# Reordering the norm steps around two MLPs and merging the attention score operations

## The reference, cut to what matters

```
x  = x + rwkv(...) @ wo                      # "wo"
x  = x + relu(rms(x) @ w1)**2 @ w2           # "mlp0": 1024 -> 4096 -> 1024
k, v = rms(x) @ w_kv ; k = rms(k)            # "kv"
q  = rms(rms(x) @ wq)                        # "q", 16 heads of 64, 2 key heads
s  = q k^T - slope_h * distance, window 128  # distance outside the window: -inf
m  = max(max(s), sink_h)
p  = exp(s - m) / (sum exp(s - m) + exp(sink_h - m))
x  = x + (p v) @ b_wo                        # "bo"
x  = x + relu(rms(x) @ w1')**2 @ w2'         # "mlp1"
ctx  = modulated(rms(context)) @ w_in[:, 512:1536]
lat  = modulated(rms(x)) @ w_in              # "qk", then v, gates, Fourier part
```

## Time and profile before

| what | us |
|---|---|
| median of 3 runs | 2321.64 (2315.77 to 2322.67) |
| the profiled execution's own time | 2319.46 |
| its span, first to last instruction | 2317.7 |
| TensorE busy | 2145.5 (93%) |
| VectorE busy | 1227.5 (53%) |
| ScalarE busy | 800.4 (35%) |
| GpSimd busy | 158.7 (7%) |

### The profile page before, as it was taken

How to read it: one execution, slowest core, us unless ns; L and a number is a source line. 1 busy time by engine, 2 the same in 40 slices (tenths; PEclk the granted TensorE clock), 3 DMA queues, 4 the chain that set the end, 5 groups by cost and what they waited for, 6 DMA issues and landing times. The chain is left out here.

```text
span 2317.7 us, 34614 instructions
## 1 busy us (share of the span) xinstructions
PE 2145.5 (93%) x14072; PEld 1639.1 (71%) x14072; DVE 1227.5 (53%) x1784; ACT 800.4 (35%) x1312; POOL 158.7 (7%) x128
## 2 busy tenths in 40 slices
PE   6999999989999999888899999998998787999997
PEld 1667899927787787556668888886874365888885
DVE  5578565563534434547637557456342645556423
ACT  5766333322312212425532122225222323444311
POOL 0000222220101101000001011010000000000000
PEclk9999999969999999999999999999999898999998
DMA  4320000032232232220035534534320012232320
GB/s 173 111 79 31 3 4 4 5 136 73 90 102 91 82 109 79 67 70 1 19 109 177 195 137 138 189 129 138 125 82 0 9 64 91 91 105 94 136 91 36
DMA packets 58499, 200.76 MB, mean 87 GB/s; under 512 B 7936, under 2 KB 10752, under 8 KB 57344
## 3 DMA queue, kind: packets, MB, share of 16 engines
q1 hardware_dynamic: 57760, 194.17, 24.5%
q10 hardware_dynamic: 608, 4.72, 0.6%
HBM read 191.92 MB, written 6.42 MB: 86 GB/s over the span
## 5 line engine op out<-in xcount | busy, mean ns | idle before, releaser
L1067 DVE TENSOR_TENSOR wlo<-raw,whi 128x1024 fp32r<-128x1024 f32 x282 | 342.2, 1223 | 705.1 <-ACT whi L622 703.7
L622 ACT ACTIVATE whi<-raw 128x1024 fp32r<-128x1024 f32 x282 | 295.3, 1057 | 852.7 <-PE bank L1684 828.3
L1682 PE MATMUL bank<-inh,whi 128*128 128x512 f32 x1200 | 473.9, 395 | 37.8 <-DVEq L1617 16.1
L1683 PE MATMUL bank<-inl,whi 128*128 128x512 f32 x1200 | 471.3, 393 | 0.0
L1684 PE MATMUL bank<-inh,wlo 128*128 128x512 f32 x1200 | 470.9, 392 | 0.0
L1682 PEld LDWEIGHTS bank<-inh,whi 128*128 128x128 f32 x1200 | 228.0, 190 | 93.7 <-DVEq L1617 16.9
L1683 PEld LDWEIGHTS bank<-inl,whi 128*128 128x128 f32 x1200 | 227.8, 190 | 48.1 <-issue 0.7
L1684 PEld LDWEIGHTS bank<-inh,wlo 128*128 128x128 f32 x1200 | 227.9, 190 | 48.0
L1682 PE MATMUL bank<-hidh,whi 128*128 128x512 f32 x576 | 231.0, 401 | 10.1 <-DVE wlo L1067 4.5
L1683 PE MATMUL bank<-hidl,whi 128*128 128x512 f32 x576 | 228.4, 397 | 0.0
L1684 PE MATMUL bank<-hidh,wlo 128*128 128x512 f32 x576 | 228.0, 396 | 0.0
(11 more groups left out here) (351 smaller groups left out, 3003.2 us busy)
## 6 DMA issues: line engine op xcount, KB each, us to landing
raw<-in_mlp_w SPq DMA_DIRECT2D x128, 512.0 KB, 3.6
ADW<-in_w_ada SPq DMA_DIRECT2D x32, 768.0 KB, 5.2
raw<-in_w_up SPq DMA_DIRECT2D x44, 512.0 KB, 3.5
raw<-in_w_in SPq DMA_DIRECT2D x28, 512.0 KB, 3.6
raw<-in_a_w_rkv SPq DMA_DIRECT2D x24, 512.0 KB, 3.3
raw<-in_w_down SPq DMA_DIRECT2D x22, 512.0 KB, 3.4
raw<-in_a_wo SPq DMA_DIRECT2D x8, 512.0 KB, 5.9
raw<-in_b_wq SPq DMA_DIRECT2D x8, 512.0 KB, 3.2
```

The lines of the kernel that those rows point to most:

```text
L622: act.activation(whi[u % SLOTS][:, :], raw[u % SLOTS][:, :], ACT.Copy).then_inc(w_hi, 1)
L1067: dve.tensor_tensor(wlo[u % SLOTS][:, :], raw[u % SLOTS][:, :], whi[u % SLOTS][:, :].bitcast(F32), ALU.subtract).then_inc(w_lo, 1)
L1682: pe.matmul(o, w[:, wc], xh, start=start, stop=False)
L1683: pe.matmul(o, w[:, wc], xl_, start=False, stop=False)
```

## The change

ScalarE makes the high part of a block before its square, and after the first four squares the high parts of the later blocks go ahead of their squares (kv: two of them). TensorE makes the sums in two groups of four, after different units. VectorE makes the low parts of blocks 0 and 1 between the additions of `add_x` (after blocks 2 and 5). mlp0 is built like mlp1 (loop of two passes, turn c written out) and the drain behind it is gone. In mlp1's turn c the modulations run after three of eight splits, and SyncE's loads of `RC` and `CX` come behind the third weight load of the down pass. The retention states come after k = 2 instead of k = 1, with banks 2 and 3 between them and the wait for their eviction. In attention the gain of q is multiplied by 1/slope, the distances are negated, and one `tensor_tensor_reduce` for each half replaces L1402, L1409 and L1412: it writes (scores + band) times -slope and the minimum of that and -sink.

```diff
-    band = np.stack([first, band, band], 1)
+    band = -np.stack([first, band, band], 1)
...
+                    if layer == 1 and tag == "c" and j == 2:
+                        sp.wait_ge(dmo.sem, dmo.at(("sum", "c", CB - 1)))
+                        sp.wait_ge(rc_out, 16)
+                        sp.dma_start(RC[:], rsp).then_inc(rc_in, 16)
+                        sp.dma_start(CX[:], t["ctx"]).then_inc(in_ctx, 16)
...
-            def x_stats(name, prev, dst, gain, last_unit, root=True):
-
-                for kb in range(CB):
+            def x_stats(name, prev, dst, gain, last_unit, order):
+
+                for what, kb in order:
                     act.wait_ge(x_sum.sem, x_done(prev, kb))
-                    square_of(name, kb, X[:, kb, :])
-                    if kb == CB - 1:
-                        act.wait_ge(lin.sem, used(last_unit, None))
-                    gained_hi(name, dst, gain, kb)
-                if root:
-                    root_of(name, PB[0])
+                    if what == "square":
+                        square_of(name, kb, X[:, kb, :])
+                    else:
+                        if kb == CB - 1:
+                            act.wait_ge(lin.sem, used(last_unit, None))
+                        gained_hi(name, dst, gain, kb)
+
+            first_half = [(what, kb) for kb in range(4) for what in ("hi", "square")]
+            inputs_first = first_half + [("hi", kb) for kb in range(4, CB)] + [("square", kb) for kb in range(4, CB)]
+            squares_first = first_half + [("hi", 4), ("hi", 5)] + [("square", kb) for kb in range(4, CB)] + [("hi", 6), ("hi", 7)]
...
+                split_run(u0, 1)
+                root_of(name, PB[0])
...
-                    split_run(u + 8, 8, lp)
+                    split_run(u + 8, 3, lp)
+                    if layer == 1 and tag == "c":
+                        modulated_hi("ctx", chh, CT, lambda kb: adac[:, kb, 1:2], CTX)
+                    split_run(u + 11, 5, lp)
...
-                        act.activation(pb, pb, ACT.Exp, bias=st[:, b:b + 1], accum_out=st[:, 2 + b:3 + b]).then_inc(aat.sem, aat.step())
+                        act.activation(pb, pb, ACT.Exp, scale=-1.0, bias=st[:, b:b + 1], accum_out=st[:, 2 + b:3 + b]).then_inc(aat.sem, aat.step())
...
+                    if follow is not None and m in (2, 5):
+                        name, dst_h, dst_l, gain = follow
+                        gained_lo(name, dst_h, dst_l, gain, (m // 3,))
...
-            def mlp(layer, u0, name, at_end=None):
-                gained_lo(name, inh, inl, f"ln_mlp{layer}")
+            def mlp(layer, u0, name, at_end=None, follow=None):
+                gained_lo(name, inh, inl, f"ln_mlp{layer}", range(2, CB))
+                split_run(u0, 1)
...
-                    split_run(u + 8, 8, lp)
-                    if tag == "c":
+                    split_run(u + 8, 3, lp)
+                    if tag == "c" and at_end is not None:
                         at_end()
-                    add_x(nm, lp)
+                    split_run(u + 11, 5, lp)
+                    add_x(nm, lp, follow if tag == "c" else None)
...
-                    dve.scalar_tensor_tensor(S1[i % 3][:].rearrange("p (a b) -> p a b", a=2), BAND[:, nn:nn + 2, :],
-                                                        -(2.0 ** (-8.0 * (h + 1) / HEADS)),
-                                                        PB[i % 4][:].rearrange("p (a b) -> p a b", a=2), ALU.mult, ALU.add).then_inc(da.sem, da.step(("taken", i)))
-                    k = da.n
-                    dve.wait_ge(da.sem, k)
                     if i >= 4:
                         dve.wait_ge(da.sem, da.at(("den", i - 4)))
-                    dve.tensor_reduce(st[:, 8:10], S1[i % 3][:].rearrange("p (a b) -> p a b", a=2), AX.X, ALU.max).then_inc(da.sem, da.step())
-                    k = da.n
-                    dve.wait_ge(da.sem, k)
-                    dve.tensor_scalar(st[:, 0:2], st[:, 8:10], col("sinks", h), -1.0, ALU.max, ALU.mult).then_inc(da.sem, da.step(("nm", i)))
+                    for b in range(2):
+                        half = slice(b * 256, (b + 1) * 256)
+                        dve.tensor_tensor_reduce(S1[i % 3][:, half], PB[i % 4][:, half], BAND[:, nn + b, :], -(2.0 ** (-8.0 * (h + 1) / HEADS)),
+                                                 SINKM[:, h:h + 1], ALU.add, ALU.min, st[:, b:b + 1]).then_inc(
+                            da.sem, da.step(*([("taken", i), ("nm", i)] if b else [])))
...
-                             late=(0,), after={0: lambda: sums4(name, PB[0]), 1: lambda: total(name, PB[0])}, late_after=rooted)
+                             late=(rooted, 0), after={(0, 7): lambda: sums4(name, PB[0], range(4)), (1, 7): lambda: sums4(name, PB[0], range(4, CB)),
+                                                      (2, 4): lambda: total(name, PB[0])})
...
-            pe.drain().then_inc(phase, 1)
-            pe.wait_ge(phase, phase_done("pe"))
...
+                    if kb == 7:
+                        total("kv", PB[0])
...
-                if j == 1:
-                    sums4("kv", PB[0])
-                if j == 2:
-                    total("kv", PB[0])
+                if j in (1, 2):
+                    sums4("kv", PB[0], range(4 * j - 4, 4 * j))
...
-                if k == 2:
+                if k == 1:
                     pe.wait_ge(x_sum.sem, x_done("mlp1c", 4))
-                    sums4("lat", PB[4])
+                if k in (1, 2):
+                    sums4("lat", PB[4], range(4 * k - 4, 4 * k))
...
-            wide(UIN, inh, inl, "qk", ready=(dad, ("lo", "lat")), free=(x_sum, lambda m: x_done("mlp1c", m)), late=(0, 1, 2, 3), after={1: states}, late_after=states_taken)
+            wide(UIN, inh, inl, "qk", ready=(dad, ("lo", "lat")), free=(x_sum, lambda m: x_done("mlp1c", m)), late=(states, 2, 3, states_taken, 0, 1))
```

More of the change, by code:

```diff
@@ L1289, in split_run, with add_x @@
                     split_lo(u + 3, loop)
-            def add_x(stage, loop=None):
+            def add_x(stage, loop=None, follow=None):
                 for m in range(CB):
@@ L1346, in work @@
                     hidden_lo(7)
-                    split_run(u + 8, 8, lp)
-                    if tag == "c":
+                    split_run(u + 8, 3, lp)
+                    if tag == "c" and at_end is not None:
                         at_end()
-                    add_x(nm, lp)
+                    split_run(u + 11, 5, lp)
+                    add_x(nm, lp, follow if tag == "c" else None)
                 work("a", u0, None)
-                with turns(dve, "dve", name, 3 - layer, 16) as lp:
+                with turns(dve, "dve", name, 2, 16) as lp:
                     lp.first = u0 + 16
                     work("b", u0 + 16, lp)
-                if layer == 1:
-                    work("c", u0 + 48, None)
+                work("c", u0 + 48, None)
             split_run(UWO, 8)
-            add_x("wo")
-            mlp(0, UM0, "mlp0")
-            dve.drain().then_inc(phase, 1)
-            dve.wait_ge(phase, phase_done("dve"))
+            add_x("wo", follow=("mlp0", inh, inl, "ln_mlp0"))
+            mlp(0, UM0, "mlp0", follow=("kv", inh, inl, "kv_norm"))
             dve.memset(QNI[:], 0.0).then_inc(dk.sem, dk.step("qnz"))
-            gained_lo("kv", inh, inl, "kv_norm")
+            gained_lo("kv", inh, inl, "kv_norm", range(2, CB))
             split_run(UKV, 1)
@@ L1476, in _ @@
             split_run(UBO, 8)
-            add_x("bo")
+            add_x("bo", follow=("mlp1", inh, inl, "ln_mlp1"))
             def modulations():
@@ L1661, in _, with sums4 @@
             pn, pl = STEP["pe_norm"], STEP["pe_lora"]
-            def sums4(name, bank):
-                for kb in range(CB):
+            def sums4(name, bank, kbs):
+                for kb in kbs:
                     g = kb % 4
@@ L1937, in _, with wide @@
             dmlp = STEP["dve_mlp"]
-            def wide(u0, mh, ml, stage, loop=None, ready=None, free=None, zero=None, late=(), after=None, late_after=None):
+            def wide(u0, mh, ml, stage, loop=None, ready=None, free=None, zero=None, late=(), after=None):
+                banks = [m for m in late if isinstance(m, int)]
                 def block_(k, m):
@@ L1955, in wide @@
                     for m in (*range(1, CB), 0) if k == 0 and zero is not None else range(CB):
-                        if not (k < 3 and m in late):
+                        if not (k < 3 and m in banks):
                             block_(k, m)
-                    if after is not None and k in after:
-                        after[k]()
-                    if k == 2 and late:
-                        late_after()
+                        if after is not None and (k, m) in after:
+                            after[k, m]()
+                    if k == 2:
                         for m in late:
-                            for k2 in range(3):
-                                block_(k2, m)
```

(24 more changed lines are left out.)

37 lines of the change are left out of this document (16 added, 21 removed).

## The result

The changed kernel takes 2267.78 us (median of 4 runs, 2265.27 to 2269.51) where the kernel before takes 2320.47 (4 runs, 2315.77 to 2322.67): a ratio of 0.9773, 95% interval 0.9761 to 0.9785. The forecast was 2267 with a range of 2259 to 2284. The profiled execution took 2269.51 us, 1.7 above the median.

A forecast was written before the change was run, and what follows sets the result against it. TensorE, busy 93% of the span, was taken as the bound, with time to be had only in its waits. Savings of 8.4 + 8.4 + 4.9 + 12.9 + 19.8 = 54.4 us take the median from 2321.64 to 2267 us, range 2259 to 2284.

The forecast's parts named there:

- A: End of wo and start of mlp0: TensorE goes straight on, sums run in two groups without waits; 8.4 us saved.
- C: End of bo and start of mlp1: same steps as at mlp0; 8.4 us saved.
- B: From mlp0 over kv to q: drain goes, new waits of 0.6, 1.0 and 1.6 us; 4.9 us saved.
- a chain that the change leaves as it is: From kv's total to q's start: root, reciprocal, three low parts, splits; 8.3 us, unchanged.
- D: mlp1 to context and states: additions start earlier, k = 2 fills the gap at the states; 12.9 us saved.
- E: Attention loop: merged operations take a pair of iterations from 6.59 to 5.35 us, 16 pairs; 19.8 us saved.
- n: Attention: time from the first merged operation to the exponentials, taken as 1.0 us with 0.43 an operation.
- free chain: Attention: VectorE and ScalarE in turn, 3.32 + n + (n - 0.1) a pair, 5.22 us.
- the forecast's bound: Attention: a bound of TensorE's own, two pairs take at least 2n + 8.7, so 5.35 us a pair.
- Half rate (1): Attention: merged operation runs at half rate, 0.70 us each, only 4.6 us saved there; 2282 us, chance 0.13.
- A boundary that gives back (2): One stage boundary loses its gain to a new wait, late weight or low clock, 5 to 9 us; 2274, chance 0.15.
- Rivals 3 and 4: Attention: merged operations at 0.78 us each gain nothing, 2287, chance 0.05; at 1.68 each they lose 58, 2345, chance 0.03.

The follow-up runs named there:

- e7: Changed kernel with all low parts of the norm inputs behind the eight additions again, at mlp0, kv and mlp1: 2277.67 us, ratio 0.9816.
- e8: Changed kernel with all eight sums behind k = 0 and squares ahead of high parts again, at mlp0 and mlp1 alone: 2272.64 us, ratio 0.9794.
- e6: Changed kernel with the context input and the loads of context and reciprocal back at the end of turn c: 2275.26 us, ratio 0.9805.
- e11: Changed kernel with kv's sums after blocks 1 and 3, total ahead of block 5, copy of sums ahead of the split: 2259.56 us, ratio 0.9733.
- e1: Changed kernel with attention's merged operations put back to the three operations of before: 2283.63 us, ratio 0.9842.
- e10: Kernel before with attention's merged operations and their constants alone: 2300.73 us, ratio 0.9912.
- e2: Changed kernel with one merged operation more in each attention iteration, its results unused: 2274.85 us, ratio 0.9798.
- e3: Changed kernel with attention's low part issued one iteration later, behind that iteration's merged operations: 2258.82 us, ratio 0.9735.
- e9: Kernel before with attention's low part issued an iteration later, the three operations kept: 2310.49 us, ratio 0.9951.
- e4: Changed kernel with 16 merged operations more behind attention's last low part, sources in PSUM or SBUF, 256 or 512 wide: 2280.88 us, one run.
- e5: Changed kernel with kv's total one block earlier, ahead of block 6 and not of block 7: 2263.49 us, ratio 0.9751.

## Why the prediction was right, and where it was not

**A and C** (8.4 each): 8.0 and 8.7. From mlp0's first product to the end of the second sums the forecast had 11.8 us; it starts at 570.93, and the sums' successor at 582.77: 11.8. e7 and e8 take the gain apart: about 4.3 us from the low parts (2.5 of it the wait, the rest the clock) and 3 to 4 from the sums.

**B** (4.9): 3.4. All three waits came, as forecast: 0.58, 0.71 and 1.81 for 0.6, 1.0 and 1.6. The step that failed is the time of "a chain that the change leaves as it is". It took 947.18 to 956.37, 9.2 us for 8.3, since its first member, the total, ran behind the wait of 1.81 at the lower clock: 1.91 us instead of 1.02, and the root began that much later. I had priced the wait and not the clock behind it. But the wait alone doesn't settle the clock: of the nine profiles with the same wait of 1.81, e6 and e8 have the total at 1.02, the chain at 8.31 and a gain of 4.5 in kv's column. So 0.9 of the missing 1.5 go with where a stretch at the lower clock fell, and what puts it there is open. The other 0.6 are in the sum up to the total: taken from mlp0's end as in the forecast it came after 15.7 us for 15.1, though the three waits together were no longer than forecast. Each delays the next start by 0.1 to 0.2 us more than the idle shown for it, since the idle counts from the end of a matmul of 0.39 us whose successor could start after 0.23. e11 shows the chain at 8.3 too. The idle ahead of q was 5.27 for "about 6.4", and 5.89 in e6 and e8, where block 7's product ran at the full clock.

**D** (12.9): 14.4. The context's total came 1551.32 - 1537.98 = 13.3 us behind mlp1 for 13.2. The gap at the states shrank by 2.76, 3.28 to 0.52, for 2.7. Not in the sum was that the states' own 32 matmuls then take 3.81 us and not 5.22: the granted clock was 0.72 there before and is 1.00 now. `RC` and `CX` on SyncE's queue cost nothing that TensorE shows, as taken: it waits for no weight there.

**E** (19.8): 19.5 in the column. The operation's price was 0.40 for my 0.43, n 0.92 for 1.0, the pair 5.385 for 5.35. e1 and e10 show the term from both sides (18.0 and 20.5), and at equal clock it is 18.0, 1.8 under the forecast: all 16 pairs were priced like the steady ones, and the first three save less. That the column still shows 19.5 is luck, 1.5 us of it with the clock.

The mechanism was right: two chains, the later counts. The free chain of 5.06 over VectorE, ScalarE and the low part is real (e2, which lengthens it, follows it to 0.01 us). The other one is the forecast's bound, and the rows of E let it be followed for two pairs: exponentials (1059.12); 1.81 later the product behind the copy `PTR` (1060.93); 3.54 later the scores after the next ones (1064.47), with TensorE busy throughout; 1.17 later VectorE's merged operation on them (1065.64); 0.93 later exponentials (1066.57); 2.40 later the end of the low part (1068.97); and 0.92 later exponentials again. The sum is 10.77, just the two pairs. In the forecast's form it is 2n + 8.92 for 2n + 8.7, whose 6.3 was 6.52 (its own terms, 1.81 + 2.49 + 0.9 + 1.0, add to 6.2); n was 0.08 too high, and the two slips nearly cancel. What was wrong is its name: it is no bound of TensorE's own, since VectorE and ScalarE have 2n + 2.4 of it. With the low part behind the next merged operations it is gone, and TensorE's own work needs 9.82 for two pairs (e3). What e9 adds: of before's 6.59 us a pair, the low part's place held 0.94 (down to 5.65), and the three operations another 0.74 (down to e3's 4.91).

**Rivals.** Half rate (1): e4 measured 0.267 us for 256 elements from both memories, so neither the 0.70 us an operation nor the 2282 of the rival could come. The Trainium skill, Vector Engine (DVE) Microarchitecture Reference, section Points that are easy to get wrong, says of the fused shape with an accumulator that two non-bf16 sources in SBUF halve its throughput; here the trace doesn't agree: 485 ns from SBUF, 484 from PSUM. It may be that this operation isn't of that shape, for the trace calls it by another name. A boundary that gives back (2): B did, 1.5 us and not 5 to 9. Rivals 3 and 4 fell with the price of 0.40.

**The sum.** 54.4 was forecast and its five stages gave 54.0, with q 54.7; by the two spans it is 50.2, of which the column ahead of wo took 3.8 back, and by the medians 52.7. That 54.4 and 54.0 lie so close is partly luck, B's 1.5 too few against D's 1.5 too many, with 1.5 of E from the clock.

## What to carry to other kernels

An idle stretch of the matrix engine can cost more than its length: the matmuls behind one of 2.5 us ran at the lower clock and took 1.8 us more, in before and in e7, and a total at the lower clock lengthened the chain behind it by 0.9. It doesn't do so every time, so compare two profiles of a stage only with the time at the lower clock beside it. In a software-pipelined loop, look first at what an engine issues between two links of the chain: one subtraction of 0.34 us, waiting for its input ahead of more urgent work, held attention back by 0.48 us a pair, and moving it cost nothing. A bound made of rows holds for the order of instructions in which they were read: write down every engine's part in it, for it goes when one of them is moved.

## What was not expected of the hardware

The merged operation is two instructions in the trace: the pass, 479 ns for 256 elements with the next one starting after 0.40 us, and a read of the accumulator of 83 ns that overlaps the next pass and so takes no time of its own. The pass itself stands 0.40 us from the next where the subtraction over the same size stands at 0.34. The exponentials start 0.92 us behind the first pass. Its price doesn't depend on where the first source lies (484 and 485 ns over 256, 751 and 752 over 512). And the length of an idle stretch alone didn't tell what clock follows: ahead of q TensorE idled 5.27 us after, 3.52 in e5 and 3.18 in e11, and was then granted 0.74, 1.00 and 0.79 of the full clock over 8 us; in the time from the total to q it was 0.69, 0.81 and 1.00, so that a slow stretch ahead of q doesn't settle it either.
